# A pooling mixer's band products taken by source tile, its channel scale and shift applied behind them, its tables loaded one stage earlier, and router logits with the weights stationary

## The chip, the core and the metric

The kernel runs on one core of one Trainium2 chip. Its time is the device time of one execution in microseconds (us), as the median of several runs. TensorE is called PE in the profile's rows (PEld is its loading of stationary weights), VectorE is DVE, ScalarE is ACT, GpSimd is POOL and SyncE is SP; SPq, ACTq and POOLq are the instructions with which these engines issue transfers.

## What is computed

Two layers of a diffusion backbone work on 512 tokens of 1024 channels. Layer 0 is an attention and retention mixer, layer 1 a pooling mixer. Each mixer is followed by a mixture of 16 experts, of which every token takes two from one group. Everything is fp32. The parts that the change touches are these:

```python
def pool_mixer(h, pool_w, pool_scale):          # h = rms_norm(x, norm_mix_w) * (1 + scale) + shift
    cs = cumulative sum of h over the tokens
    for gi, w in enumerate((2, 4, 8, 16)):      # 256 channels each
        mean = (sl[:, hi] - sl[:, lo]) / (hi - lo)      # centred window of w tokens, cut at the ends
        groups.append(mean - h of these channels)
    mixed = jnp.einsum('btgc,gcd->btgd', pooled, pool_w).reshape(b, t, d)
    return mixed * pool_scale                   # x = x + g1 * mixed

def moe_route(flat, router_w, router_b):        # flat = modulate(rms_norm(x, norm_ffn_w), shift, scale)
    s = jax.nn.sigmoid((flat @ router_w).astype(jnp.float32))
    biased = s + router_b
    ...                                         # best group, its top two experts, their weights
```

## The kernel before

The program is a row of stages, and each ends with a barrier of all engines (`stage_over`). Inside a stage every engine works through its own list in the written order and waits for semaphores. The stages are: mixer of layer 0 with the routing front of its mixture (`front0`), mixture 0 (`moe(0)`), the pooling stage with `front1`, mixture 1 (`moe(1)`), and a last stage that adds the experts' results and applies the final norm.

In a mixture SP streams 48 matrices of expert weights in halves of 1 MB through a ring in SBUF (`put_half`), 414 GB/s while it runs. Its last half is issued long before the last expert is computed, and the experts' results go to a DRAM buffer (`y_scratch`) from ACT's queue.

The pooling stage does this. POOL issues eight indirect gathers (`Combine.fetch`, two per token tile of 128 rows, 512 KB each), and DVE adds each to the residual stream `x_res` (`Combine.add`, two operations per tile). ACT squares each tile and sums its squares, POOL makes the reciprocal root of it (`rstd_of`), and DVE applies it with the norm weight and the scale row and then adds the shift row (two operations per tile into `xhat`). The rows of scale, shift and norm weight are broadcast to all partitions. DVE then folds the gate row and `pool_scale` into the mixing weights `pool_w`. The pooling itself is a banded matrix of 512x512 per window, and PE multiplies with it: `xhat` is stationary, a 128x128 block of the band is moving. For each of 8 channel tiles k and each of 4 target tiles it takes the two or three source tiles that are near, 80 products in all, after a wait for all four tiles of `xhat`. Four PSUM banks are used in turn, and ACT copies each result to `pooledT`. The mixing products (`pool_w`, 32 of 256 columns) follow, DVE adds their results to `x_res`, and then `front1` runs.

A front (class `Front`) does for each tile: square on ACT, root on POOL, two operations of norm on DVE, 8 transposes on PE (`transposes`), one copy on ACT (`copy_T`, into `hT`), and 8 products with the router's weights (`logits`: 128 columns of `hT` are stationary and the 16 columns of `router_w` move). After the fourth tile ACT takes the sigmoid of a 128x64 block in PSUM (`scores`), which ends the stage. SP stores `xhat` to DRAM and loads the front's rows and tables and the first six halves of the next mixture's weights. The engine profile counts two records of PE for each fp32 product, and one for a transpose.

Two regions of SBUF have several uses: `shared` is one, and `arena` is what a stage takes beyond it.

## Time and profile before

| what | value |
|---|---|
| time, median of 3 runs | 1220.41 us (1220.31 to 1221.9) |
| the profiled execution: its time, and the span of its engines | 1222.1 us, 1220.2 us |
| share of the span in which engines are busy | PE 85%, PEld 66%, DVE 77%, ACT 50%, POOL 14% |
| mean granted clock of PE | 0.925 of full speed |
| mixture 0 begins, pooling stage begins | 458.69 us, 781.16 us |
| mixture 1 begins, last stage begins | 870.26 us, 1193.14 us |

The shares are means over stages of different kinds. In the two mixtures PE is busy nearly throughout. Between them lies a stretch of 89 us with a share of 2 to 3 tenths of PE in its first half. Times of single rows are counted from the span's start. The granted clock is 1.00 at 2.4 GHz and 0.50 at 1.2 GHz.

### The profile page before, as it was taken

How to read it: one execution, taken by the hardware profiler on the slowest of the kernel's cores; microseconds unless marked ns; L12 is line 12 of the kernel's file. 1: busy time of each engine (PE TensorE's matmuls, PEld its weight loads, DVE VectorE, ACT ScalarE, POOL GpSimd, SP SyncE). 2: the span in 40 equal slices, each digit the busy share in tenths (PEclk: the TensorE clock that was granted, in tenths of full speed). 3: DMA queues.
4: the chain of work that ended last, by engine and by line, in shares of the span. 5: the costliest groups of instructions: out<-in, count | busy, mean ns of one | idle time of the engine just before them, and what ended most of it. 6: DMA issues, size and time to landing. Idle time of an engine off the chain costs nothing. (4 is left out here: it accounts for less than half of the span.)

```text
span 1220.2 us, 13889 instructions
## 1 busy us (share of the span) xinstructions
PE 1039.8 (85%) x4830; PEld 802.0 (66%) x4830; DVE 935.0 (77%) x1042; ACT 605.2 (50%) x614; POOL 166.7 (14%) x172
## 2 busy tenths in 40 slices
PE   6789999997898983999999999239579999999970
PEld 1576767774565452788888888138558888888860
DVE  5578888964993337799999998273569999999955
ACT  1534222222663122777777776023347777777731
POOL 0100200000100004410000000221063211221005
PEclk9899999997999985999999999659579999999995
DMA  9625798555014024999999997494179999999936
GB/s 372 241 69 211 257 326 311 206 207 224 10 60 129 35 100 136 292 411 413 415 413 414 413 414 312 145 352 140 52 227 392 413 414 415 413 414 414 413 128 229
DMA packets 142861, 334.14 MB, mean 274 GB/s; under 512 B 10848, under 2 KB 12840, under 8 KB 142688
## 3 DMA queue, kind: packets, MB, share of 16 engines
q1 hardware_dynamic: 122936, 279.69, 60.5%
q10 hardware_dynamic: 12392, 28.68, 6.3%
q0 software_dynamic: 7488, 25.19, 5.4%
q8 instruction: 26, 0.43, 0.2%
q14 instruction: 19, 0.16, 0.0%
HBM read 310.42 MB, written 23.15 MB: 273 GB/s over the span
## 5 line engine op out<-in xcount | busy, mean ns | idle before, releaser
L1828 DVE TENSOR_TENSOR w_lo<-ring,w_hi 128x2048 fp32r<-128x2048 f32 x192 | 431.3, 2285 | 25.4 <-ACT w_hi L1674 22.1
L1674 ACT CAST w_hi<-ring 128x2048 fp32r<-128x2048 f32 x192 | 365.8, 1914 | 131.6 <-DMA ring<-in_moe_w_up 50.2
L1919 PE MATMUL bank<-w_hi,xT_hi 128*128 128x512 f32 x512 | 205.2, 401 | 8.1 <-DVE xT_lo L1835 8.1
L1919 PE MATMUL bank<-w_hi,xT_lo 128*128 128x512 f32 x512 | 201.5, 394 | 0.0
L1919 PE MATMUL bank<-w_lo,xT_hi 128*128 128x512 f32 x512 | 201.1, 393 | 0.0
L1368 PE MATMUL bank<-ring_last_parts,arena_parts 128*128 128x512 f32 (+1 forms) x320 | 117.7, 398 | 5.4 <-DVE ring_parts L988 2.7
L1919 PEld LDWEIGHTS bank<-w_hi,xT_hi 128*128 128x128 f32 x512 | 97.3, 190 | 29.4 <-DVE xT_lo L1835 9.8
L1919 PEld LDWEIGHTS bank<-w_hi,xT_lo 128*128 128x128 f32 x512 | 97.1, 190 | 21.2
L1919 PEld LDWEIGHTS bank<-w_lo,xT_hi 128*128 128x128 f32 x512 | 97.5, 190 | 19.4
L1046 DVE SCALAR_TENSOR_TENSOR gate_b<-ring,silu_c,gate_b 128x512 f32<-128x512 f32 x140 | 105.9, 756 | 4.5
L1934 PE MATMUL bank<-w_hi,hT_hi 128*128 128x512 f32 x256 | 101.2, 395 | 7.5 <-DVE w_lo L1828 7.5
L1934 PE MATMUL bank<-w_hi,hT_lo 128*128 128x512 f32 x256 | 100.8, 394 | 0.0
L1934 PE MATMUL bank<-w_lo,hT_hi 128*128 128x512 f32 x256 | 100.6, 393 | 0.0
L1368 PE MATMUL bank<-ring_parts,arena_parts 128*128 128x512 f32 (+1 forms) x256 | 100.6, 393 | 0.0
L1368 PEld LDWEIGHTS bank<-ring_last_parts,arena_parts 128*128 128x128 f32 x320 | 60.4, 192 | 31.6 <-issue 13.1
L1368 PE MATMUL bank<-ring_last_parts,x_parts 128*128 128x512 f32 x192 | 77.3, 403 | 0.0
L1631 POOL DMA_INDIRECT shared<-xh_scratch,shared x32 | 62.9, 1966 | 63.9 <-DVE shared L1819 55.8
L1934 PEld LDWEIGHTS bank<-w_hi,hT_hi 128*128 128x128 f32 x256 | 48.9, 191 | 18.1 <-issue 7.9
L741 ACT CAST ring_last_parts<-ring 128x1024 fp32r<-128x1024 f32 x24 | 25.2, 1050 | 68.7 <-PE bank L1368 63.1
L1661 POOL CAST shared<-shared 128x1 uint32<-128x1 int32 x26 | 11.2, 431 | 329.0 <-PE bank L1902 323.0
L1934 PEld LDWEIGHTS bank<-w_lo,hT_hi 128*128 128x128 f32 x256 | 48.9, 191 | 10.2
L1934 PEld LDWEIGHTS bank<-w_hi,hT_lo 128*128 128x128 f32 x256 | 48.6, 190 | 10.3
(246 smaller groups left out, 1425.5 us busy)
## 6 DMA issues: line engine op xcount, KB each, us to landing
ring<-in_moe_w_gate SPq DMA_DIRECT2D x64, 1024.0 KB, 11.5
ring<-in_moe_w_up SPq DMA_DIRECT2D x64, 1024.0 KB, 13.4
ring<-in_moe_w_down SPq DMA_DIRECT2D x64, 1024.0 KB, 11.1
ring<-in_ada_w SPq DMA_DIRECT2D x21, 2048.0 KB, 8.7
y_scratch<-shared ACTq DMA_DIRECT2D x32, 512.0 KB, 6.0
ring<-in_w_in ACTq DMA_DIRECT2D x21, 512.0 KB, 3.8
shared<-in_ada_w SPq DMA_DIRECT2D x2, 2048.0 KB, 16.0
x_res<-in_x SPq DMA_DIRECT2D x8, 512.0 KB, 12.4
```

The costliest lines, as they stand in the source:

```text
L741: nc.scalar.copy(w_high(n), w_raw(n)).then_inc(m_whi, 1)
L1046: ins = nc.vector.scalar_tensor_tensor(ada_acc[:, i % 2, :], w[:, k, :], silu_c[:, 0, k:k + 1], onto, ALU.mult, ALU.add)
L1368: last = pe.matmul(acc(u)[:, c0:c1], hs[h_], ws[w_], start=(kk == 0 and i == 0), stop=(kk == KD - 1 and i == 2))
L1631: pool.indirect_dma_start(out=xg[:, u, :], out_offset=None, in_=xh_dram, in_offset=bass.IndirectOffsetOnAxis(ap=idx[:, c:c + 1], axis=0)). ...
L1661: nc.gpsimd.tensor_copy(idx[:, u:u + 1], lists[:, m:m + 1]).then_inc(s_idx, 1)
L1674: nc.scalar.copy(w_hi[:, buf(u, p), :], half(raw(e, p))).then_inc(s_hi, 3 if isinstance(e, int) and (e, p) == (-1, 3) else 1)
L1828: V.tensor_tensor(w_lo[:, buf(u, p), :], half(raw(e, p)), w_hi[:, buf(u, p), :].bitcast(F32), ALU.subtract).then_inc(s_lo, 3 if isinstance ...
L1919: last = pe.matmul(bank[:, b, :], xs[:, kk, :], ws[:, k, :], start=(kk == 0 and i == 0), stop=(kk == KD - 1 and i == 2))
L1934: last = pe.matmul(bank[:, 6 + hf, :], xs[:, kk, :], ws[:, k, at], start=(kk == 0 and i == 0), stop=(kk == KE - 1 and i == 2))
```

## The change

The change has five parts.

1. The band products go by source tile. For each source tile t, as soon as its `xhat` is there, PE multiplies it, for each of the 8 channel tiles, with the 128 rows of the band that belong to it, 135 to 143 columns wide (`band_range`), and adds into eight PSUM banks. That makes 32 products.
2. The norm before them is one operation on ACT (`normed`, x times the reciprocal root). Scale, norm weight and shift act per channel, and channels are the partitions of the result, so they are applied where it is copied out of PSUM: four banks by ACT, four by DVE (`BY_ACT`, `BY_DVE`). The shift is multiplied with the mean column sum of the bands (`k_band_sum`).
3. Bands, raw `pool_w`, gate row and the three vectors in column form are loaded by SP at the end of mixture 0, into free parts of `shared` and `mod`. The column loads take elements of 4 bytes, 1024 of them in each of three. SP waits for all seven loads in that stage.
4. In the pooling stage DVE folds the gate before its adds, then does its eight adds in one run. SP loads the front's rows and tables before the six weight halves and not between them. PE puts the first transposes of the front ahead of the last mixing products, and runs logits(t) right behind transposes(t).
5. In both fronts the router's weights (16 columns) are stationary and 128 columns of `hT` move. The result lies by expert. ACT takes the sigmoid of 16x512, PE turns it back with four transposes (`scores_T`), and DVE copies 128x64 to `score` (`copy_scores`), which ends the stage.

```diff
+BAND_W = P + max(WINDOWS) - 1
+def band_range(t):
+    return max(t * P - (max(WINDOWS) // 2 - 1), 0), min((t + 1) * P + max(WINDOWS) // 2, SEQ)
...
             def scores(self, act):
                 act.wait_ge(self.lg, NT)
-                nc.scalar.activation(self.at.score..., bank[:, self.LOGITS, 0:NT * NE], ACT.Sigmoid).then_inc(self.done, 1)
+                nc.scalar.activation(self.by_expert, bank[0:NE, self.LOGITS, :], ACT.Sigmoid).then_inc(self.sg, 1)
+            def scores_T(self, pe):
+                pe.wait_ge(self.sg, 1)
+                for t in range(NT):
+                    last = pe.transpose(bank[:, self.SCORES, t * NE:(t + 1) * NE], self.by_expert[:, t * P:(t + 1) * P],
+                                        ident[0:NE, 0:NE])
+                last.then_inc(self.sgt, 1)
+            def copy_scores(self, dve):
+                dve.wait_ge(self.sgt, 1)
+                nc.vector.tensor_copy(self.at.score..., bank[:, self.SCORES, 0:NT * NE]).then_inc(self.done, 1)
...
                 for k in range(KD):
-                    last = pe.matmul(bank[:, self.LOGITS, t * NE:(t + 1) * NE], self.at.hT[:, k, t * P:(t + 1) * P],
-                                     self.at.router_w[:, k, :], start=(k == 0), stop=(k == KD - 1))
+                    last = pe.matmul(bank[0:NE, self.LOGITS, t * P:(t + 1) * P], self.at.router_w[:, k, :],
+                                     self.at.hT[:, k, t * P:(t + 1) * P], start=(k == 0), stop=(k == KD - 1))
...
# mixture 0, SP, behind the last halves of the expert weights
+                    if l == 0:
+                        sp.dma_start(bands..., a["k_bands"]).then_inc(s_pool, 16)
+                        sp.dma_start(pool_w_raw..., a["pool_w"][0]...).then_inc(s_pool, 16)
+                        sp.dma_start(gate1_b[:], mod_row(1, G1)).then_inc(s_pool, 16)
+                        for i, src in enumerate((mod_dram[1, SC1 * D:(SC1 + 1) * D], mod_dram[1, SH1 * D:(SH1 + 1) * D],
+                                                 a["norm_mix_w"][1])):
+                            sp.dma_start(pool_cols[:, i * KD:(i + 1) * KD], src.rearrange("(k p) -> p k", p=P)
+                                         ).then_inc(s_pool, 16)
+                        sp.dma_start(pool_cols[:, 3 * KD:3 * KD + 1], a["k_band_sum"]).then_inc(s_pool, 16)
+                        sp.wait_ge(s_pool, 16 * 7)
...
# pooling stage, SP
+                sp.dma_start(pool_scale, a["pool_scale"][0].partition_broadcast(P)).then_inc(p_ps, 16)
+                sp.wait_ge(p_wg, 1)
                 sp.wait_ge(combine.done, NT - 1)
...
                 front1.load_rows(sp)
                 front1.load_tables(sp)
+                sp.wait_ge(combine.done, NT)
+                for r in range(6):
                     put_half(sp, 1, 0, r)
...
# pooling stage, ACT: squares(0), squares(1), normed(0), squares(2), normed(1), squares(3), normed(2), normed(3), then
+                for k in BY_ACT:
+                    act.wait_ge(p_pl, K_ORDER.index(k) + 1)
+                    nc.scalar.activation(pooledT[:, k, :], bank[:, k, :], ACT.Identity, scale=scale_c[:, k:k + 1],
+                                         bias=shift_c[:, k:k + 1]).then_inc(p_ea, 1)
...
# pooling stage, DVE: the two column vectors, the gate, all adds, then
                 front1.scales(dve)
+                for k in BY_DVE:
+                    dve.wait_ge(p_pl, K_ORDER.index(k) + 1)
+                    nc.vector.tensor_scalar(pooledT[:, k, :], bank[:, k, :], scale_c[:, k:k + 1], shift_c[:, k:k + 1],
+                                            ALU.mult, ALU.add).then_inc(p_ed, 1)
...
# pooling stage, PE
-                pe.wait_ge(p_ld, 32)
-                pe.wait_ge(p_xh, NT)
-                for k in range(KD):
...
+                for t in range(NT):
+                    pe.wait_ge(p_xh, t + 1)
+                    lo, hi = band_range(t)
+                    for k in K_ORDER:
+                        last = pe.matmul(bank[:, k, lo:hi], xhat[:, t, k * P:(k + 1) * P], bands[:, k // 2, t, 0:hi - lo],
+                                         start=(t == 0), stop=(t == NT - 1), skip_group_check=True)
...
+                for t in range(3):
+                    mix(t)
+                front1.transposes(pe, 0)
+                mix(3)
+                front1.logits(pe, 0)
+                for t in range(1, NT):
                     front1.transposes(pe, t)
-                    if t >= 1:
-                        front1.logits(pe, t - 1)
-                front1.logits(pe, NT - 1)
+                    front1.logits(pe, t)
+                front1.scores_T(pe)
```

PE's list in the pooling stage, before; L2246 are band products, L2257 mixing products, L318 the transposes and L328 the logits of `front1`.

```order
L2246 MATMUL bank<-arena 128x128 x80
L2257 MATMUL bank<-arena 128x256 x32
L318 MATMUL bank<-ident,shared 128x128 x16
L328 MATMUL bank<-shared 128x16 x8
L318 MATMUL bank<-ident,shared 128x128 x8
L328 MATMUL bank<-shared 128x16 x8
L318 MATMUL bank<-ident,shared 128x128 x8
L328 MATMUL bank<-shared 128x16 x16
```

The same place in the changed program; L2284 are band products, L2300 mixing products, L343 transposes, L353 logits and L305 the transposes of the scores.

```order
L2284 MATMUL bank<-shared,arena 128x136 x8
L2284 MATMUL bank<-shared,arena 128x143 x16
L2284 MATMUL bank<-shared,arena 128x135 x8
L2300 MATMUL bank<-arena 128x256 x24
L343 MATMUL bank<-ident,shared 128x128 x8
L2300 MATMUL bank<-arena 128x256 x8
L353 MATMUL bank<-shared 16x128 x8
L343 MATMUL bank<-ident,shared 128x128 x8
L353 MATMUL bank<-shared 16x128 x8
```

The first transposes moved ahead of the last 8 mixing products, each tile's logits stand right behind its transposes, and 80 band products became 32.

DVE's list at the head of the pooling stage, before; L2119 are the adds, L2206 the scale row, L2212 and L2214 the norm, L2218 and L2221 the gate, L298 the front's scale row.

```order
L2119 SCALAR_TENSOR_TENSOR x_res<-shared,weight,x_res 128x1024 x4
L2206 SCALAR_TENSOR_TENSOR arena<-arena 128x1024
L2119 SCALAR_TENSOR_TENSOR x_res<-shared,weight,x_res 128x1024 x2
L2212 SCALAR_TENSOR_TENSOR arena<-x_res,rstd,arena 128x1024
L2214 TENSOR_TENSOR arena<-arena 128x1024
L2119 SCALAR_TENSOR_TENSOR x_res<-shared,weight,x_res 128x1024 x2
```

The same place in the changed program; L2252 and L2253 are the column vectors, L2255 and L2257 the gate, L2163 the adds, L323 the front's scale row and L2266 the copies out of PSUM.

```order
L2252 SCALAR_TENSOR_TENSOR mod<-mod 128x8
L2253 TENSOR_SCALAR mod<-mod 128x8
L2255 TENSOR_TENSOR gate_b<-gate_b,arena 128x1024
L2257 TENSOR_TENSOR arena<-shared,gate_b 128x4x256 x2
L2163 SCALAR_TENSOR_TENSOR x_res<-arena,weight,x_res 128x1024 x8
L323 SCALAR_TENSOR_TENSOR shared<-shared,arena 128x1024
L2266 TENSOR_SCALAR arena<-bank,mod 128x512 x4
```

The gate moved ahead of the adds, the four norms left DVE, and the front's scale row stands ahead of DVE's four copies.

## Rows read from the trace of the kernel before

**Rows 1.** Timeline, pooling stage: start, length, engine, line, operation, idle before.

```profile
781.16 0.34 SPq L2154 DMA_DIRECT2D arena<-mod_scratch  x1
791.24 1.28 DVE L2119 SCALAR_TENSOR_TENSOR x_res<-shared,weight,x_res 128x1024 f32<-128x1024 f32 x1 [15.61 <-DMA shared<-y_scratch,row_of]
801.19 1.06 ACT L2178 ACTIVATE arena<-x_res 128x1024 f32<-128x1024 f32 x1 [2.75 <-DVE x_res L2119]
802.70 1.44 POOL L212 TENSOR_TENSOR rstd<-rstd,minus_half 128x1 f32<-128x1 f32 x1
803.65 2.60 DVE L2119 SCALAR_TENSOR_TENSOR x_res<-shared,weight,x_res 128x1024 f32<-128x1024 f32 x2
812.51 1.23 DVE L2214 TENSOR_TENSOR arena<-arena 128x1024 f32<-128x1024 f32 x1
813.89 20.12 PE L2246 MATMUL bank<-arena 128*128 128x128 f32 x160 [39.51 <-DVE arena L2214]
834.05 0.59 ACT L2182 COPY arena<-bank 128x512 f32<-128x512 f32 x1 [1.65 <-PE bank L2246]
```

**Rows 2.** Timeline, mixing products and front, to mixture 1's first transfer.

```profile
834.68 14.08 PE L2257 MATMUL bank<-arena 128*128 128x256 f32 x64 [0.68 <-ACT arena L2182]
848.60 1.04 PE L318 MATMUL bank<-ident,shared 128*128 128x128 f32 x8
849.67 1.01 ACT L277 COPY shared<-bank 128x1024 f32<-128x1024 f32 x1 [5.37 <-PE bank L318]
861.73 6.85 PE L328 MATMUL bank<-shared 128*128 128x16 f32 x32
868.61 0.22 ACT L287 ACTIVATE shared<-bank 128x64 f32<-128x64 f32 x1 [4.11 <-PE bank L328]
870.26 0.32 SPq L1615 DMA_DIRECT2D gate_b<-mod_scratch  x1
```

**Rows 3.** Gathers of the pooling stage: issues first and last, time to landing.

```profile
L2104 POOL DMA_INDIRECT shared<-y_scratch,row_of x8: 933/938/940, 782.4 to 791.1; - x8
...
DMA to landing us min/median/max: 8.9/9.5/9.6
```

**Rows 4.** Gathers of the last stage, time to landing.

```profile
DMA to landing us min/median/max: 4.7/5.6/5.9
```

**Rows 5.** The last stage's only other load (512 KB, final norm weight), time to landing.

```profile
DMA to landing us min/median/max: 3.3/3.3/3.3
```

**Rows 6.** Windows: length, busy PE, PEld, DVE, ACT, POOL, clock, DMA share, GB/s.

```profile
444.50:447.20 2.70, 0.01 (x1) 0.00 (x0) 0.60 (x1) 2.05 (x3) 0.74 (x2) 1.00 0.00 0
447.20:449.20 2.00, 1.96 (x16) 1.86 (x16) 1.94 (x2) 0.00 (x0) 0.00 (x0) 1.00 0.00 0
813.80:818.00 4.20, 4.11 (x19) 4.14 (x20) 3.44 (x3) 0.00 (x0) 0.00 (x0) 0.50 1.05 405
848.70:855.30 6.60, 3.72 (x34) 3.41 (x32) 4.09 (x4) 4.12 (x6) 1.93 (x3) 1.00 0.19 79
855.30:858.00 2.70, 2.70 (x15) 2.70 (x16) 2.02 (x2) 1.01 (x1) 0.55 (x1) 0.57 0.47 194
```

**Rows 7.** Timeline, end of the first front: last logits and sigmoid.

```profile
452.89 3.59 PE L328 MATMUL bank<-shared 128*128 128x16 f32 x16 [1.10 <-ACT shared L277]
456.52 0.22 ACT L287 ACTIVATE shared<-bank 128x64 f32<-128x64 f32 x1 [2.17 <-PE bank L328]
```

**Rows 8.** Timeline, mixture 0: SP's last weight half, ACT's last store.

```profile
746.33 0.38 SPq L450 DMA_DIRECT2D ring<-in_moe_w_down  x1
...
775.67 0.34 ACTq L1694 DMA_DIRECT2D y_scratch<-shared  x1
```

**Rows 9.** Page, DMA issues: count, KB each, median us from issue to landing.

```profile
ring<-in_moe_w_down SPq DMA_DIRECT2D x64, 1024.0 KB, 11.1
```

**Rows 10.** DMA view, 825 to 827 us, tables of the front: packets by size.

```profile
DMA packets 1613, 0.44 MB, mean 222 GB/s; under 512 B 1411, under 2 KB 1542, under 8 KB 1613
```

**Rows 11.** Scatters of token numbers into the lists: 128 four-byte elements each.

```profile
DMA to landing us min/median/max: 2.6/8.9/12.5
```

More of the change, by code:

```diff
@@ L83, in constants @@
             full[t, t] -= 1.0
-        for b, (a, t) in enumerate([(0, 0), (1, 1), (NT - 1, NT - 1), (0, 1), (2, 1)]):
-            bands[:, g, b] = full[a * P:(a + 1) * P, t * P:(t + 1) * P]
+        band_sum += full.sum(0).mean()
+        for t in range(NT):
+            lo, hi = band_range(t)
+            bands[:, g, t, 0:hi - lo] = full[t * P:(t + 1) * P, lo:hi]
     rows = np.zeros((2, NE), np.float32)
@@ L94, in constants @@
         "k_ages": np.ascontiguousarray(ages.reshape(P, -1), np.float32),
-        "k_bands": bands.reshape(P, -1), "k_rows": rows, "k_token": np.ascontiguousarray(token),
+        "k_bands": bands.reshape(P, -1), "k_band_sum": np.full((P, 1), band_sum, np.float32), "k_rows": rows, "k_token": np.ascontiguousarray(token),
         "k_places": np.arange(P, dtype=np.float32)[None, :],
@@ L2123, in build_program @@
         moe(0)
-        stage_memory(14000 + 17000)
-        rows, at = carve(0, 2, NT, D)
-        combine = Combine("combine0", rows)
+        stage_memory(33500)
         normw_ffn, at = carve(14000, D)
@@ L2131, in build_program @@
         assert front1.at.end <= 14000
-        bands, at = carve(at, len(WINDOWS), 5, P)
+        rows, at = carve(at, 2, NT, D)
+        combine = Combine("combine0", rows)
         pool_w, at = carve(at, len(WINDOWS), 2, 2 * P)
@@ L2175, in _, with squares @@
             def _(act):
-                for t in range(NT):
+                def squares(t):
                     act.wait_ge(combine.done, t + 1)
@@ L2179, in _, with normed @@
                                          accum_out=stats[:, t:t + 1]).then_inc(p_sq, 1)
-                for k in range(KD):
-                    act.wait_ge(p_pl, k + 1)
-                    nc.scalar.copy(pooledT[:, k, :], bank[:, k % 4, :]).then_inc(p_plc, 1)
+                def normed(t):
+                    act.wait_ge(p_rs, t + 1)
+                    nc.scalar.activation(xhat[:, t, :], x[:, t, :], ACT.Identity, scale=rstd[:, t:t + 1]).then_inc(p_xh, 1)
+                squares(0)
+                squares(1)
+                normed(0)
+                squares(2)
+                normed(1)
+                squares(3)
+                normed(2)
+                normed(3)
+                act.wait_ge(p_cs, 1)
+                for k in BY_ACT:
+                    act.wait_ge(p_pl, K_ORDER.index(k) + 1)
+                    nc.scalar.activation(pooledT[:, k, :], bank[:, k, :], ACT.Identity, scale=scale_c[:, k:k + 1],
+                                         bias=shift_c[:, k:k + 1]).then_inc(p_ea, 1)
                 for t in range(NT):
@@ L2232, in _, with mix @@
                 front1.norm(dve, NT - 1)
+                front1.copy_scores(dve)
             @block.tensor
             def _(pe):
-                pe.wait_ge(p_ld, 32)
-                pe.wait_ge(p_xh, NT)
-                for k in range(KD):
-                    if k >= 4:
-                        pe.wait_ge(p_plc, k - 3)
-                    g = k // 2
-                    for t in range(NT):
-                        near = [(t2, b) for t2, b in ((t - 1, 3), (t, 0 if t == 0 else 2 if t == NT - 1 else 1), (t + 1, 4))
-                                if 0 <= t2 < NT]
-                        for n, (t2, b) in enumerate(near):
-                            last = pe.matmul(bank[:, k % 4, t * P:(t + 1) * P], xhat[:, t2, k * P:(k + 1) * P],
-                                             bands[:, g, b, :], start=(n == 0), stop=(n == len(near) - 1))
-                    last.then_inc(p_pl, 1)
-                pe.wait_ge(p_plc, KD)
-                pe.wait_ge(p_wg, 1)
-                for t in range(NT):
+                for t in range(NT):
+                    pe.wait_ge(p_xh, t + 1)
+                    lo, hi = band_range(t)
+                    for k in K_ORDER:
+                        last = pe.matmul(bank[:, k, lo:hi], xhat[:, t, k * P:(k + 1) * P], bands[:, k // 2, t, 0:hi - lo],
+                                         start=(t == 0), stop=(t == NT - 1), skip_group_check=True)
+                        if t == NT - 1:
+                            last.then_inc(p_pl, 1)
+                def mix(t):
+                    if t == 0:
+                        pe.wait_ge(p_wg, 1)
                     if t >= 2:
```

82 lines of the change are left out of this document (38 added, 44 removed).

## The prediction

> **What bounds the kernel now.** I read the page first: PE is busy in 85% of the span, and its slices dip twice, at the first front and in the stretch between the mixtures. Then I read the timeline of that stretch, since the change lies almost wholly in it. The pooling stage lasts from 781.16 to 870.26 [rows 1, 2], 89.1 us, and each step in it waits for the one before. The reader should follow it as a chain. The first gather's rows reach DVE at 791.24. DVE's adds are cut up by norms that wait for POOL, so that the last add ends at 803.65 + 2.60 = 806.25 and the last norm at 813.7. Only then does PE begin, after 39.51 us of idleness [rows 1]. The band products take 20.12 us, and the last copy out of PSUM starts when they end, at 834.05. The mixing products take 14.08 us, and from their end at 848.76 it is 20.1 us to the end of the sigmoid at 868.83 [rows 2]. Nothing in this stage covers anything else for long, so a shorter chain shortens the kernel. The weights of mixture 1 are no limit: they are loaded in the same stage, and mixture 1 starts only at the barrier.
>
> The windows show PE's clock [rows 6]. It is granted at 0.50 while the band products begin, for 4.1 us, and the products behind them take half as long each. It is full until 855.3 and falls in the front's tail, before 858. In the first front PE did nothing from 444.5 to 447.2 and still had the full clock, and again in the next window with its 16-column products; the last products there, 16 records in 3.59 us, ran slow (224 ns each against 123) [rows 6, 7].
>
> **The change part by part**, as times on the old time axis.
>
> *Adds.* The load of `pool_scale` lands 3.3 us after its issue if it is like the last stage's lone load [rows 5]: 784.5. Three gate operations of 1.23 us (the 128x1024 operation of DVE in rows 1) end at 788.2. The old stage loads three rows beside its gathers, the new one loads one, as the last stage does; there the gathers land after 4.7 to 5.9 us instead of 8.9 to 9.6 [rows 3, 4]. So the first is there at 787.1 to 788.3, and the last, issued at 791.1, at 797.0. Eight adds of 1.30 us [rows 1] run from 788.3 to 798.7, and the gate is hidden in the wait for the gathers. If the gathers landed as late as before, the last add would end at 791.1 + 9.6 + 1.3 = 802.0. I take the first, since the traffic is that of the last stage.
>
> *Norm.* Per tile ACT squares (1.06 us and 0.19 to read the sum) and applies the root (no row has this operation; the square has its shape and one input, so 1.06; the copy of 1.01 [rows 2] is the lower end). POOL's root takes 0.19 + 1.44 us [rows 1]. ACT interleaves them, and with POOL busy issuing until 792 to 794.5 the four tiles are ready at about 797.4, 799.6, 801.8 and 803.7, the last one 10 us sooner than before.
>
> *Band products.* 160 records were made for 80 products. In the slow window 19 take 4.11 us, 216 ns each; the other 141 take 16.0 us, 113 ns each [rows 1, 6]. A product of 139 columns in the mean instead of 128 costs two records times 1.09: 0.47 us slow, 0.25 fast, so 8 of them 3.8 or 2.0. Tile 0 runs slow from 797.4 to 801.2. If the clock rises 4.1 us after the start, as it did, tile 1 ends at 803.4, tile 2 at 805.4 and tile 3 at 807.4. A rise one tile later costs 1.7. Copies go on ACT and DVE side by side: 0.59 for a bank on ACT [rows 1], half of 1.23 on DVE. Two of them fit beside two products, so the mixing products start at about 807.4, where they started at 834.68: 27.3 us gained. DVE's copies stand behind the front's scale row, which waits for three loads issued at about 796.5. At 3.3 us they cost nothing, at the 9.6 of a crowded queue 807 + 1.3 = 808.3 is the first copy's start, 2.5 us late. I take 0.
>
> *Mixing products.* 14.1 us as before, but the first transposes now stand ahead of the last eight. They wait for add 1 (1.2) and norm 0 (two operations, 2.5) behind the second tile's products, which end at 814.6: ready at 818.6, where PE has been free since 818.0. With 1.04 for themselves they add 1.7. The mixing ends at 823.2, 25.6 us sooner than before.
>
> *Tail.* Logits now move 128 columns, 8 products of 2 x 113 ns, 1.8 us; the old ones took 1.96 for 16 records and were set by loading 128 columns of weights (PEld 1.86 of 2.00) [rows 6]. So at full clock the swap itself is worth almost nothing. A round is transposes 1.04 with 0.25 until ACT sees them, copy 1.01, hand-over 0.1, logits 1.8: 4.2 us. Logits 0 and three rounds end at 823.2 + 1.8 + 12.6 = 837.6. Then come the new steps: a sigmoid of 512 columns for 64 (at most the bank copy's 0.59), four transposes (half of 1.04), a copy of 128x64 (0.22 as on ACT, at least nothing), and three hand-overs of 0.1: 1.6 us. The barrier took 870.26 - 868.83 = 1.4. The stage ends at 840.6, a gain of 29.7.
>
> *The clock in the tail.* This sum has PE at full clock to the end. What stood before both falls in the old trace were products of 16 moving columns; both are gone. A pause alone did not lower it from 444.5 to 447.2. The Trainium skill, "TensorE: Matmul & The Clock Gate", Part 1, has the clock fall after an idle window. By that rule too it would stay up here, since no pause of PE in a round is longer than 1.4 us; but the old tail fell without long idleness, so the rule alone is not enough.
>
> *First front.* Old: the last logits began at 452.89 after a pause of 1.10, so the transposes ended at 451.8 and, slow, took about twice 1.04 from 449.7; slow logits 3.59, sigmoid until 456.74 [rows 7]. New at full clock: transposes to 450.8 (the norm before them ends when it did), copy to 451.9, logits 1.8 and hand-over to 454.0, new steps 1.6: 455.6. That gains 1.1. At the slow clock nothing is saved and the new steps cost 1.5.
>
> *Tables in mixture 0.* SP's last weight half is issued at 746.33 [rows 8] and lands after 11.1 us [rows 9]: 757.4. Behind it come 2.74 MB, 6.8 us at 405 GB/s [rows 6]: 764.2. The column loads are 3,200 packets of 4 bytes, 200 for each of 16 DMA engines. In two microseconds of the front's tables 1,411 small packets went through [rows 10], 22.7 ns per packet and engine: 4.5 us, so 768.7. ACT issues its last store at 775.67 [rows 8], and the barrier comes later still. The loads are hidden behind the last expert with 7 us to spare, up to 57 ns per packet. The other end is the scatter of four-byte elements: 8 packets per engine in 8.9 us [rows 11], 1.1 us each, 222 us in all. That is a software queue's whole latency and not a packet's cost, and I stay with the tables. The Trainium skill, "DMA: Bandwidth & Descriptors", Specifications, says that below 512 B a write becomes read-modify-write and misses line rate. It gives no price that I use; the rule speaks for a packet dearer than mine, and its effect is the late-tables rival.
>
> *Mixture 1.* Its six halves are issued after the last add, behind 1.8 MB of rows and tables, from about 803. 8 MB at 405 GB/s is 20 us: 823, and the barrier is at 840. Its inside does not change.
>
> **Sum.** 29.7 + 1.1 = 30.8, less 0.5 for a clock that may rise late: 30.3. The profiled execution took 1222.1 with a span of 1220.2; the median of the runs, 1220.41, is 1.7 below it, and the gain is taken from the median: 1190.
>
> **Rivals.**
> - Clock falls in the tail. Each of three rounds then costs 2.0 for 1.04 and 3.5 for 1.8, 2.6 more, with the last transposes 8.2 in all, and the first front loses 1.5 instead of gaining 1.1. Time 1200.5, or 1194 and up if it falls late. For it: PE still pauses 1.4 us in each round. Against it: fuller products. Chance 0.15.
> - DVE or loads late (gathers as slow as before, or the scale row's loads at 9.6 us): 2.5 to 3.5 more, 1193 to 1194. Chance 0.11.
> - Tables late but bearable: 60 to 200 ns per packet hold the barrier of mixture 0 for 1 to 28 us, 1191 to 1218. Chance 0.03.
> - No gain: the weights of mixture 1 would have to land as late as 870. Nothing in the rows says so. Chance 0.005.
> - Slower than before: four-byte packets above 57 + 30,300/200 = 209 ns. At the scatter's 1.1 us the tables would end at 986 and the time be near 1400. Chance 0.005.
> - The forecast, 1186 to 1193, has the rest, 0.70.
>
> **How the numbers follow.** About 0.2% (2.4 us) is what a measurement here can tell from no change. All likely cases are beyond it: faster 0.985, same 0.005, slower 0.01. The range takes in the forecast, late loads and most of the clock case: 1185.5 to 1198. It leaves out the deepest slow tail and late tables.
>
> **What the new trace would show.** Right: DVE's adds in one run ending near 799; PE's first band product near 797; mixing from 807 to 823; logits records of about 113 ns to the end with clock 1.00; stage end near 840; mixture 0's end unmoved at 781. Wrong if PE sits before the mixing for DVE's scale row, if the last logits take 3.5 us per tile, or if SP holds the barrier of mixture 0.

## The result: 29.6 us faster, as forecast

| kernel | median us (lowest to highest, runs) | ratio to before, 95% interval |
|---|---|---|
| before | 1221.16 (1220.31 to 1222.41, 4) | |
| changed | 1191.53 (1190.79 to 1191.72, 4) | 0.976 [0.9746, 0.9774] |

The forecast was 1190.0 and its range 1185.5 to 1198. The profiled execution has a span of 1189.6 us, where before had 1220.2, and a mean granted clock of 0.939. PE's line on the page:

```profile
PE 1025.7 (86%) x4742; PEld 781.1 (66%) x4742; DVE 929.3 (78%) x1041; ACT 607.9 (51%) x614; POOL 137.7 (12%) x172
```

The stages, each counted from its first transfer to that of the next, show where the time came from:

| stage | before, us | changed, us | gain |
|---|---|---|---|
| up to mixture 0 | 458.69 | 456.68 | 2.0 |
| mixture 0 | 322.47 | 323.51 | -1.0 |
| pooling stage with the front | 89.10 | 58.94 | 30.2 |
| mixture 1 | 322.88 | 323.78 | -0.9 |
| last stage | 27.06 | 26.69 | 0.4 |

The first row and the two mixtures differ between profiles of kernels that are the same there: mixture 0 began between 456.68 and 459.80 us in the eleven profiles with the new logits and took 322.34 to 323.55 us. So only the third row is clear of that scatter. It divides into three parts:

| pooling stage | before, us | changed, us | gain |
|---|---|---|---|
| stage begins to first band product | 32.73 | 15.48 | 17.25 |
| first band product to first mixing product | 20.79 | 11.17 | 9.6 |
| first mixing product to the stage's end | 35.58 | 32.29 | 3.3 |

The timeline of the changed pooling stage, first half, answers to [rows 1]. Columns are start, length, engine, line, operation and the idle time before it.

```profile
784.58 1.23 DVE L2255 TENSOR_TENSOR gate_b<-gate_b,arena 128x1024 f32<-128x1024 f32 x1 [4.04 <-DMA arena<-in_pool_scale]
...
788.12 10.66 DVE L2163 SCALAR_TENSOR_TENSOR x_res<-arena,weight,x_res 128x1024 f32<-128x1024 f32 x8
...
790.67 0.94 POOL L2148 DMA_INDIRECT arena<-y_scratch,row_of  x1 [0.30 <-issue]
790.79 1.06 ACT L2211 ACTIVATE arena<-x_res 128x1024 f32<-128x1024 f32 x1 [26.50 <-DVE x_res L2163]
...
792.31 1.52 POOL L222 TENSOR_TENSOR rstd<-rstd,minus_half 128x1 f32<-128x1 f32 x1
...
794.49 1.13 ACT L2216 ACTIVATE arena<-x_res,rstd 128x1024 f32<-128x1024 f32 x1
...
795.67 10.73 PE L2284 MATMUL bank<-shared,arena 128*128 128x136 f32 x64 [22.29 <-ACT arena L2216]
...
801.59 1.22 DVE L323 SCALAR_TENSOR_TENSOR shared<-shared,arena 128x1024 f32<-128x1024 f32 x1 [2.81 <-DMA arena<-in_norm_ffn_w]
...
804.90 2.79 ACT L2229 ACTIVATE arena<-bank,mod 128x512 f32<-128x512 f32 x4 [2.84 <-PE bank L2284]
805.16 2.97 DVE L2266 TENSOR_SCALAR arena<-bank,mod 128x512 f32<-128x512 f32 x4 [2.35 <-PE bank L2284]
...
806.84 10.60 PE L2300 MATMUL bank<-arena 128*128 128x256 f32 x48 [0.43 <-DVE arena L2266]
```

The eight adds are one row without a gap, so no gather made DVE wait. PE starts 15.5 us after the stage begins, where before it took 32.7. While PE works through the band products, ACT's norms of the later tiles go on beside it. DVE's idle time of 2.81 us ahead of L323 looks like a late load, but it costs nothing: DVE would otherwise have waited for PE's banks, which it does right behind, for 2.35 us.

The second half answers to [rows 2]; L353 are the logits, L305 turns the scores back.

```profile
817.75 1.09 PE L343 MATMUL bank<-ident,shared 128*128 128x128 f32 x8 [0.32 <-DVE shared L334]
...
818.68 3.62 PE L2300 MATMUL bank<-arena 128*128 128x256 f32 x16
818.88 1.01 ACT L289 COPY shared<-bank 128x1024 f32<-128x1024 f32 x1 [2.46 <-PE bank L343]
...
822.23 1.92 PE L353 MATMUL bank<-shared 128*16 128x128 f32 x16
...
826.28 1.92 PE L353 MATMUL bank<-shared 128*16 128x128 f32 x16 [1.10 <-ACT shared L289]
...
834.37 1.92 PE L353 MATMUL bank<-shared 128*16 128x128 f32 x16 [1.10 <-ACT shared L289]
...
836.33 0.59 ACT L299 ACTIVATE shared<-bank 16x512 f32<-16x512 f32 x1 [0.49 <-PE bank L353]
...
836.97 0.41 PE L305 MATMUL bank<-ident,shared 16*128 16x16 f32 x4 [0.68 <-ACT shared L299]
837.42 0.22 DVE L312 COPY shared<-bank 128x64 f32<-128x64 f32 x1 [6.66 <-PE bank L305]
...
839.13 0.32 SPq L1648 DMA_DIRECT2D gate_b<-mod_scratch  x1
```

Each round of the tail repeats after 4.05 us: transposes, a wait of 1.10 for ACT's copy, logits. The logits keep 1.92 us to the last, where the old tail ended with 32 records in 6.85 us [rows 2]. The windows of the changed kernel give the clock (columns as in [rows 6]):

```profile
796.00:801.00 5.00, 5.00 (x23) 5.00 (x23) 2.61 (x3) 4.38 (x7) 2.98 (x5) 0.50 0.79 255
801.00:802.00 1.00, 1.00 (x8) 1.00 (x7) 0.41 (x1) 1.00 (x1) 0.00 (x0) 0.71 1.01 341
...
822.30:836.30 14.00, 10.69 (x89) 8.38 (x88) 6.15 (x5) 5.57 (x7) 0.74 (x2) 1.00 0.27 109
```

It is half for the first 5.9 us of band products (0.71 in the second window puts the rise at 801.6) and full through the whole tail.

### The profile page after: what moved, and what is told of

Read it like the earlier page. It is cut to its first block and busy times, and to the rows that moved or that the text cites. A ratio compares the mean times of both kernels' runs of the same rounds, so it can differ in the third digit from the quotient of the medians.

```text
span 1189.6 us, 13716 instructions
## 1 busy us (share of the span) xinstructions
PE 1025.7 (86%) x4742; PEld 781.1 (66%) x4742; DVE 929.3 (78%) x1041; ACT 607.9 (51%) x614; POOL 137.7 (12%) x172
## 5 line engine op out<-in xcount | busy, mean ns | idle before, releaser
L1896 DVE TENSOR_TENSOR shared<-bank,gate_b 128x1024 f32<-128x1024 f32 x32 | 39.0, 1219 | 21.1 <-PE bank L1978 21.1
L1394 PEld LDWEIGHTS bank<-ring_parts,arena_parts 128*128 128x128 f32 x256 | 48.5, 189 | 8.6
```

Source lines behind the costliest of these rows:

```text
L1394: last = pe.matmul(acc(u)[:, c0:c1], hs[h_], ws[w_], start=(kk == 0 and i == 0), stop=(kk == KD - 1 and i == 2))
L1896: V.tensor_tensor(y_sb[:, u, :], bank[:, 6:8, :].rearrange("p b c -> p (b c)"), gate2_b[:], ALU.mult).then_inc(s_y, 1)
```

## The experiments

Ratios are to the kernel before, which ran on the same chip beside them: 1221.42 us for the one with the gate behind the adds, the last version and the repeat, 1220.39 for the other four of the first five, 1220.24 for the rest. "Stage" is the pooling stage, 89.10 us before and 58.94 changed. Differences of a few us are read from it, since the rest of the program varies by one to three microseconds from one profile to the next. The stage has a scatter of its own: the clock rose 3.3 to 5.9 us after the first band product, 5.9 in the changed kernel's profile and 4.4 in its repeat, whose stage is 58.07 us. From the first mixing product to the stage's end both take 32.29 us. Where an edit lies in that part, this shorter count is given too, as the length from the mixing on.

### The logits form in the kernel before

```diff
 # kernel before, Front.logits
-    last = pe.matmul(bank[:, self.LOGITS, t * NE:(t + 1) * NE], self.at.hT[:, k, t * P:(t + 1) * P],
-                     self.at.router_w[:, k, :], start=(k == 0), stop=(k == KD - 1))
+    last = pe.matmul(bank[0:NE, self.LOGITS, t * P:(t + 1) * P], self.at.router_w[:, k, :],
+                     self.at.hT[:, k, t * P:(t + 1) * P], start=(k == 0), stop=(k == KD - 1))
 # and scores, scores_T, copy_scores as in part 5
```

> The kernel before with part 5 alone: router weights stationary in both fronts, sigmoid by expert, four transposes and a copy behind it; the rest is as before. Theory A (the old 16-column products are what let PE's clock fall and kept it low until the end; the new ones do not): in front 1 the last 32 records of logits take 3.6 us instead of 6.85, the stage ends 3 to 4 us sooner although the new steps cost 1.6, and with the first front the kernel gains 4 to 5 us, near 1216. Theory B (the clock follows PE's pauses whatever the products): it falls at the same place but climbs back sooner, gain 1 to 3 us. Theory C (the form of the products does nothing to the clock): two fronts pay 1.2 to 1.6 us each for the new steps, 2.5 to 3 us slower than before.

Measured: 1216.53 us, ratio 0.9968 [0.9957, 0.9979]; stage 84.82, 4.3 us shorter. Its tail and a window over it:

```profile
858.20 3.67 PE L343 MATMUL bank<-shared 128*16 128x128 f32 x32
```

```profile
848.00:862.00 14.00, 10.83 (x91) 8.56 (x89) 5.95 (x5) 7.73 (x11) 2.48 (x4) 1.00 0.27 112
```

The last 32 records take 3.67 us for 6.85, at a clock that stays at 1.00 in this tail. Here L343 is the line of the logits. The order of PE's list is that of before and it waits for the same engines, so in this tail the form of the logits keeps the clock. The length from the mixing on is 31.40 us for 35.58. One profile could owe this to chance, but the mean granted clock of all ten executions is 0.932 to 0.936, where the thirteen of the kernel before beside them have 0.922 to 0.929.

### The changed kernel with the old logits

```diff
-    last = pe.matmul(bank[0:NE, self.LOGITS, t * P:(t + 1) * P], self.at.router_w[:, k, :],
-                     self.at.hT[:, k, t * P:(t + 1) * P], start=(k == 0), stop=(k == KD - 1))
+    last = pe.matmul(bank[:, self.LOGITS, t * NE:(t + 1) * NE], self.at.hT[:, k, t * P:(t + 1) * P],
+                     self.at.router_w[:, k, :], start=(k == 0), stop=(k == KD - 1))
 # scores as before; scores_T and copy_scores gone
```

> The changed kernel without part 5: 128 columns of hT stationary again, sigmoid straight to the scores. Theory A: the clock falls in the tail of the pooling stage once the 16-column products begin, the last rounds run at 0.50, and the kernel is 4 to 7 us slower than the changed one (1196 to 1198). Theory C: it saves the new steps in both fronts and is 2 to 3 us faster than the changed one (about 1189).

Measured: 1193.46 us, ratio 0.9783 [0.9764, 0.9802]; stage 61.61, 2.7 us longer than the changed kernel's. The last logits and the windows over the tail:

```profile
836.30 3.60 PE L340 MATMUL bank<-shared 128*128 128x16 f32 x16 [1.10 <-ACT shared L289]
```

```profile
822.00:826.00 4.00, 2.90 (x26) 2.66 (x26) 3.07 (x3) 1.96 (x3) 0.00 (x0) 1.00 0.28 113
826.00:829.00 3.00, 2.71 (x18) 2.31 (x17) 1.92 (x2) 0.35 (x3) 0.74 (x2) 0.68 0.40 165
829.00:840.00 11.00, 8.98 (x40) 8.47 (x40) 0.59 (x1) 3.32 (x5) 0.00 (x0) 0.50 0.12 49
```

With 16 moving columns the clock falls and does not come back, though the pauses are the same 1.10 us. The length from the mixing on is 35.65 us, 3.4 longer. The two experiments confirm each other: in all eleven profiles with the new logits the last logits of this tail ran at full clock, and in both with the old ones at half. The mean granted clock of the four executions here is 0.929 to 0.930, of the changed kernel's four 0.937 to 0.939. The price is smaller than the 4 to 7 us that I expected. The clock fell only between 826 and 829, with part of the tail done, and the old form needs no steps that turn the scores back.

### The tables loaded in the pooling stage

```diff
 # mixture 0, SP: the seven loads and their wait are gone
 # pooling stage, SP, behind pool_scale
+    sp.dma_start(gate1_b[:], mod_row(1, G1)).then_inc(p_gt, 16)
+    sp.dma_start(pool_w_raw..., a["pool_w"][0]...).then_inc(p_gt, 16)
+    sp.dma_start(bands..., a["k_bands"]).then_inc(p_bd, 16)
+    # the three column loads and k_band_sum: p_col
 # DVE
     dve.wait_ge(p_ps, 16)
+    dve.wait_ge(p_gt, 32)           # gate and pool_w, ahead of the adds
+    # behind the adds: dve.wait_ge(p_col, 16 * 4), then the two column vectors
 # PE, ahead of the band products
+    pe.wait_ge(p_bd, 16)
```

> The changed kernel with the seven table loads issued at the start of the pooling stage, behind pool_scale, instead of at the end of mixture 0. Theory 1 (the early load is worth its place): 2.2 MB of gate, weights and bands share the queues with the gathers, the gate is folded and the adds start 3 us later, the band products wait for bands; 3 to 6 us slower than the changed kernel, 1195 to 1197. Theory 2 (the loads were hidden anyway, as DVE has 8 us of idleness there): within 1 us. If the extra 1.0 us of mixture 0 comes from the table loads, mixture 0 is back at 322.5 us here; if it comes from the clock's phase it need not be.

Measured: 1206.81 us, ratio 0.9885 [0.9863, 0.9908]; stage 75.61, so 16.7 us longer where I expected 3 to 6. This was a miss of mine:

```profile
801.99 1.23 DVE L2252 TENSOR_TENSOR gate_b<-gate_b,arena 128x1024 f32<-128x1024 f32 x1 [26.89 <-DMA shared<-in_pool_w]
```

The gate stands ahead of DVE's adds, and it waits for `pool_w` until 801.99. Everything behind it is late by that much. Mixture 0 without the loads is no shorter (323.55 us).

### Those tables, with the gate behind the adds

The miss left open whether the place of the gate costs the 16.7 us or the transfers themselves.

```diff
 # previous kernel, DVE
+    for t in range(NT):
+        combine.add(dve, t)
     dve.wait_ge(p_ps, 16)
     dve.wait_ge(p_gt, 32)
     ...                              # gate, pool_w
-    for t in range(NT):
-        combine.add(dve, t)
```

> The kernel of run e3 (all tables loaded in the pooling stage) with DVE folding the gate behind its eight adds instead of ahead of them, since in e3 the adds waited 27 us for the weights. If e3's 16.7 us were mostly the gate standing in front of the adds, the adds now end near 803 when the shared queues are empty, the mixing starts near 810, and the kernel comes out near 1195 to 1198. If it was the transfers themselves, it stays above 1203.

Measured: 1202.47 us, ratio 0.9845 [0.9829, 0.9861]; stage 70.79.

```profile
790.10 1.28 DVE L2152 SCALAR_TENSOR_TENSOR x_res<-arena,weight,x_res 128x1024 f32<-128x1024 f32 x1 [14.64 <-DMA arena<-y_scratch,row_of]
...
804.75 9.46 PE L2285 MATMUL bank<-shared,arena 128*128 128x136 f32 x64 [30.55 <-DMA shared<-k_bands]
...
814.77 1.22 DVE L323 SCALAR_TENSOR_TENSOR shared<-shared,arena 128x1024 f32<-128x1024 f32 x1 [5.23 <-DMA arena<-in_norm_ffn_w]
...
817.79 4.51 PE L2301 MATMUL bank<-arena 128*128 128x256 f32 x12 [3.58 <-DVE arena L2266]
```

Three waits for transfers take the place of one: the adds come singly, each behind its gather; PE waits for the bands until 804.75; and DVE's scale row, ahead of its copies, comes late, so that the mixing waits until 817.79. Behind that pause of 3.58 us the clock fell, to 0.50 from 819 to 821, and the 48 records of mixing took 12.29 us for 10.60. The time lies between my two forecasts, 1195 to 1198 and above 1203, so neither was right. Of the 16.7 us, 4.8 are the gate's place and 11.9 the transfers, 1.7 of these by the clock; each is sure to about a microsecond, the scatter of the clock's rise. That is what the loads in mixture 0 are worth with this order of work.

### Twelve more column loads in mixture 0

```diff
+    for i in range(12):
+        spare, _ = carve(9968 + i * KD, KD)
+        sp.dma_start(spare, mod_dram[1, SC1 * D:(SC1 + 1) * D].rearrange("(k p) -> p k", p=P)).then_inc(s_pool, 16)
-    sp.wait_ge(s_pool, 16 * 7)
+    sp.wait_ge(s_pool, 16 * 19)
```

> The changed kernel with 12 more column loads of 1024 elements of 4 bytes each behind the three, into words that nobody reads. It prices a four-byte packet. At 22.7 ns per packet and DMA engine (the prediction's price) they add 17 us of transfers, which end near 780, some 2 to 4 us behind the barrier's old place: 1193 to 1196. At 53 ns (3.4 us per load, the time SP spent on issuing one) they add 41 us, the barrier of mixture 0 moves by 25 us: about 1216.

Measured: 1191.82 us, ratio 0.9772 [0.9752, 0.9793]; stage 58.98, mixture 0 323.44 us. First the changed kernel, issues of SP and ACT at the end of mixture 0, then the windows of the experiment:

```profile
744.27 0.38 SPq L475 DMA_DIRECT2D ring<-in_moe_w_down  x1
...
745.68 9.33 SPq L1664 DMA_DIRECT2D gate_b<-mod_scratch  x1
...
755.06 3.49 SPq L1667 DMA_DIRECT2D mod<-mod_scratch  x2
758.59 3.36 SPq L1667 DMA_DIRECT2D mod<-in_norm_mix_w  x1
...
774.68 0.34 ACTq L1738 DMA_DIRECT2D y_scratch<-shared  x1
```

```profile
767.00:769.00 2.00, 2.00 (x6) 1.61 (x5) 0.15 (x1) 0.00 (x0) 0.00 (x0) 0.50 0.83 6
769.00:771.00 2.00, 2.00 (x6) 1.55 (x5) 0.00 (x0) 0.00 (x0) 0.00 (x0) 0.51 0.70 5
771.00:773.00 2.00, 2.00 (x10) 1.60 (x10) 0.00 (x0) 0.00 (x0) 0.00 (x0) 1.00 0.23 2
```

The DMA engines are busy for 0.7 to 0.8 of the time while 5 or 6 GB/s move: these are the packets of 4 bytes. 12,288 of them, 768 for each engine, run between 761 and 772 us. That is at most some 14 ns each, where I had reckoned 22.7; SP issued the twelve loads in 9.31 us, so its issue may be the limit. Both my prices, and with them both forecasts, were too high. Even five times the column loads end ahead of the barrier, and the kernel's time does not change.

### Band products after all four norms

```diff
+    pe.wait_ge(p_xh, NT)
     for t in range(NT):
-        pe.wait_ge(p_xh, t + 1)
         lo, hi = band_range(t)
```

> The changed kernel, but PE waits for all four tiles of xhat before its first band product; nothing else is changed. If what part 1 gives is the overlap of products with norms, PE starts at about 802.2 instead of 795.7, pays its 4 us at the low clock after that, and the mixing starts 5 to 6 us later: 1196 to 1198. If the gain is only in the number of products (32 for 80) and the start does not matter, since another wait ends last before the mixing, it stays within 1 us of the changed kernel.

Measured: 1197.45 us, ratio 0.9814 [0.9792, 0.9837]; stage 65.13, 6.2 us longer. PE's first band product comes 22.1 us into the stage instead of 15.5:

```profile
803.16 5.19 PE L2284 MATMUL bank<-shared,arena 128*128 128x136 f32 x21 [28.89 <-ACT arena L2216]
```

The mixing begins 32.8 us into the stage for 26.7 in the changed kernel and 25.8 in its repeat. So the overlap of norms and band products is worth 6 to 7 of the 30 us. Here nothing overlaps, and from the first band product to the first mixing product it is still 10.75 us for the 20.79 of before. So some 10 us come from the smaller number of products and the copies on two engines. No run takes these two apart or alone; the figure is read from the rows.

### The norm on DVE

```diff
 # DVE, in place of ACT's normed(t): after add(t + 2)
+    dve.wait_ge(p_rs, t + 1)
+    nc.vector.tensor_scalar(xhat[:, t, :], x[:, t, :], rstd[:, t:t + 1], None, ALU.mult).then_inc(p_xh, 1)
```

> The changed kernel with the one-operation norm on DVE, between its adds as before, and ACT only squaring. If moving the norm to ACT is a part of the gain, DVE again waits for POOL's root between adds, the last tile of xhat is 2 to 4 us late and the time is 1193 to 1195. If ACT was the bound there (2.2 us per tile against DVE's 2.6 for two adds), it is within 1 us.

Measured: 1191.8 us, ratio 0.977 [0.9747, 0.9793]; stage 58.97, the same. On DVE the operation takes 0.76 us, on ACT 1.13. PE began 1.2 us later than in the changed kernel (16.7 us into the stage), but the clock rose 3.5 us after that and not 5.9, and the mixing began at the same 26.7. Against the repeat, which began it at 25.8, it is 0.9 late. So moving the norm to ACT gained less than a microsecond, if anything. That it became one operation probably gained more, since two of 1.28 and 1.22 us stood in its place; no run shows that alone.

### PE's old order in the tail

```diff
-    for t in range(3):
-        mix(t)
-    front1.transposes(pe, 0)
-    mix(3)
-    front1.logits(pe, 0)
-    for t in range(1, NT):
+    for t in range(NT):
+        mix(t)
+    for t in range(NT):
         front1.transposes(pe, t)
-        front1.logits(pe, t)
+        if t >= 1:
+            front1.logits(pe, t - 1)
+    front1.logits(pe, NT - 1)
```

> The changed kernel with PE's old order in the mixing and front: all four mixing tiles, then transposes(t) and logits(t-1) in turn. Theory 1 (the new order of part 4 buys 2 us or more by letting ACT's copy and the squares go sooner): 1193.5 or more. Theory 2 (what it gives by the early copy it loses again, since transposes in the mixing cost 1.1 to 1.7 us and PE pauses 1.1 us per round for ACT's copy, where the old order has the logits of the tile before): within 1 us of the changed kernel, 1190.5 to 1192.5.

Measured: 1189.64 us, ratio 0.9751 [0.9728, 0.9773]; stage 57.64, 1.3 us shorter than the changed kernel's.

```profile
806.72 14.05 PE L2300 MATMUL bank<-arena 128*128 128x256 f32 x64 [0.43 <-DVE arena L2266]
...
831.56 3.67 PE L353 MATMUL bank<-shared 128*16 128x128 f32 x32
```

Mixing runs unbroken, and the logits of one tile lie in the wait for the copy of the next. The order that came with part 4 costs 0.9 us: the length from the mixing on is 31.35 here and 32.29 in both profiles of the changed kernel. The rest of the 1.3 us by the stages is the clock's earlier rise in the band products. The medians agree in sign (1.9 us, below both my ranges), but they come from two chips, and the intervals of the ratios overlap. The first experiment, with the same order and the same logits, has nearly the same length (31.40).

### Two pairs of banks for the transposes

```diff
 # Front: odd tiles of front1 transpose into banks 4 and 5
+    def t_bank(self, t):
+        return 4 if self.l and t % 2 else 0
 # transposes
-    if t >= 1:
-        pe.wait_ge(self.hta, t)
+    if t >= (2 if self.l else 1):
+        pe.wait_ge(self.hta, t - 1 if self.l else t)
 # ACT: the square of tile 3 ahead of the copy of tile 1
 # PE: mix 0 to 2, transposes 0, mix 3, logits 0, transposes 1, then transposes(t), logits(t - 1), and logits 3
```

> The changed kernel with the rounds of front 1 taken apart: odd tiles are transposed into the mixing's banks 4 and 5, so that transposes no longer wait for ACT's copy; PE does logits(t-1) behind transposes(t); ACT squares tile 3 ahead of its copy of tile 1. If the tail is a round trip PE to ACT to PE of 4.05 us per tile, the last logits end 2 to 3 us sooner: 1188.5 to 1189.5. If DVE's norms (2.5 us per tile and an add) bound it, less than 1 us.

Measured: 1188.59 us, ratio 0.9745 [0.9722, 0.9768]; stage 56.64, 2.3 us shorter, and the length from the mixing on is 30.03 for 32.29. The ratios alone do not tell it from the changed kernel.

```profile
826.73 1.09 PE L349 MATMUL bank<-ident,shared 128*128 128x128 f32 x8 [0.90 <-DVE shared L339]
...
829.99 1.09 PE L349 MATMUL bank<-ident,shared 128*128 128x128 f32 x8 [0.32 <-DVE shared L339]
```

The wait for the copy is gone. The transposes of the last two tiles now wait for DVE's norm.

### The same, with all mixing products first

```diff
-    for t in range(3):
+    for t in range(NT):
         mix(t)
     front1.transposes(pe, 0)
-    mix(3)
-    front1.logits(pe, 0)
     front1.transposes(pe, 1)
+    front1.logits(pe, 0)
 # ACT: squares 0, 1, 2 ahead of the first copy
```

> Run e7 with all four mixing tiles ahead of the first transposes (what e6 showed to be the better order) and the square of tile 2 ahead of the copy of tile 0: mixing ends near 821, tile 3's norm 2.5 us later than tile 2's, last logits near 832.5 instead of 834.6. Expected 1186 to 1187.5; if DVE's chain of add and norm per tile still sets the end as in e7, no better than e7 (1188.6).

Measured: 1187.73 us (1184.33 to 1190.78, 5 runs), ratio 0.9718 [0.9704, 0.9733]; stage 55.64, length from the mixing on 28.88. The median is just above my range. The changed kernel was run once more beside it:

> The changed kernel itself once more, on the same chip as the two above, to compare them without the scatter between chips: ratio 0.976 to the kernel before, as in the first measurement; its first front and the last expert of mixture 0 may show the low clock at other places, which moves the time by 1 us.

Measured: 1190.3 us (1190.12 to 1193.19, 5 runs), ratio 0.9757 [0.9743, 0.977]; stage 58.07. The intervals do not touch. This version is 0.4% faster than the changed kernel, 2.6 us by the medians, 2.4 by the stages and 3.4 by the length from the mixing on (its clock rose late in the band products, after 5.7 us), and its median is the lowest of the study.

## Why the prediction was right, point by point

Times here are from the start of the pooling stage, which was 781.16 on the axis of the prediction and 780.19 in the changed trace.

| step | predicted | measured |
|---|---|---|
| gate begins | 3.3 | 4.4 |
| last add ends | 17.5 | 18.6 |
| first band product | 16.2 | 15.5 |
| mixing begins | 26.2 | 26.7 |
| mixing ends | 42.0 | 42.1 |
| one round of the tail | 4.2 | 4.05 |
| from the last logits to the barrier's end | 3.0 | 2.8 |
| stage | 59.4 | 58.9 |

- **Adds.** `pool_scale` took 1.1 us longer to land than the last stage's lone load [rows 5], and the whole run moved by that. The step that mattered, gathers as early as in the last stage [rows 4], held: they landed after 6.0 us (median of eight), and the adds ran without a gap.
- **Norm.** The square and the norm of the first tile were done sooner than I reckoned, since POOL had issued its last gather at 791.61 and began the root at once, where I had it busy until 792 to 794.5. ACT's norm took 1.13 us for the estimated 1.06. PE began 0.7 us sooner and then stood at the low clock for 5.9 us where I had 4.1, so nothing was left of it. This is the late rise for which the sum had 0.5 us. In the repeat it came after 4.4 us, and the mixing began at 25.8.
- **Mixing.** The first transposes ahead of the last eight products were ready at 817.75; PE had closed its 24 products (48 records) at 817.44. A record of the mixing products takes 0.22 us as before. The interruption cost 1.4 us (15.46 for 14.05), where I had 1.7.
- **Tail.** Three rounds at 4.05 instead of 4.2 give the half microsecond by which the stage is shorter than predicted. The new steps behind the logits are as estimated: 0.59, 0.41 and 0.22 us of work and the hand-overs. That the clock stays up was the step with the most doubt, with a chance of 0.15 against it. The first two experiments show that in this tail the form of the logits decides it, in this order of PE's list and in the old one.
- **First front.** The term that was mis-sized. Transposes of the third tile to the barrier took 15.21 us before and 14.70 in the changed kernel, a gain of 0.5 and not 1.1. After a pause of 2.72 us the clock did fall here, and it came back behind the new logits:

```profile
445.74 2.81 PE L353 MATMUL bank<-shared 128*16 128x128 f32 x16 [2.72 <-ACT shared L289]
448.48 1.81 PE L343 MATMUL bank<-ident,shared 128*128 128x128 f32 x8
...
451.40 1.92 PE L353 MATMUL bank<-shared 128*16 128x128 f32 x16 [1.10 <-ACT shared L289]
...
453.36 0.59 ACT L299 ACTIVATE shared<-bank 16x512 f32<-16x512 f32 x1 [0.49 <-PE bank L353]
```

  Logits of 2.81 and transposes of 1.81 us are slow ones, the last 1.92 is at full clock, where the last of before took 3.59 [rows 7]. In the kernel with PE's old order, whose first front is the same, the pause was 2.72 us too and the clock did not fall, and the stretch took 13.81. In the one with two bank pairs it took 15.42. So this gain lies between -0.2 and 1.4 us. Of the eleven profiles with the new logits four kept the clock in this front (13.81 or 13.82 us), and in seven it fell, in four behind the pause of 2.72 us and in three behind the one of 1.10 (14.40 to 15.42 us). In both with the old logits it fell. So the new form, which kept the clock in every tail, does not keep it here. The other 1.5 us of the 2.0 up to mixture 0 lie ahead of the changed code. The same pause of 2.72 us thus let the clock fall in some profiles and not in others. The Trainium skill, "TensorE: Matmul & The Clock Gate", Part 1, says that the gate's phase is not tied to the kernel, so that the same program meets it at different places from run to run; these profiles agree with that. The same part ties the fall to idleness. That rule alone, as the prediction said, is not enough: in the second experiment it fell with pauses of 1.10 us, and the tail of the first experiment has longer ones (up to 1.53) and full clock. In the old tail it fell in the transposes behind a pause of 1.69 us, which took 1.64 us for 1.06 (kernel before):

```profile
855.28 1.64 PE L318 MATMUL bank<-ident,shared 128*128 128x128 f32 x8 [1.69 <-DVE shared L309]
```

- **Tables.** Mixture 0 hides them with more room than I gave: the last column load has landed at 763.9 and the last small table at 765.3, not 768.7, and both table rivals are excluded up to five times the column loads. SP's issue of the gate row took 9.33 us (L1664 above), presumably because the transfers ahead of it filled the queue. It costs nothing, since SP has nothing else to do.
- **Mixtures.** I had their inside unchanged, but each was a microsecond longer in the changed trace. The windows over mixture 0 and over its last expert, of the changed kernel and then of its repeat:

```profile
456.68:780.19 323.51, 291.83 (x1354) 242.30 (x1354) 283.64 (x244) 213.66 (x145) 37.67 (x39) 0.94 0.92 354
763.00:771.00 8.00, 6.15 (x15) 4.87 (x16) 3.90 (x2) 1.29 (x1) 0.00 (x0) 0.57 0.21 66
```

```profile
457.55:779.89 322.34, 290.65 (x1354) 241.52 (x1354) 283.58 (x244) 215.53 (x145) 59.62 (x39) 0.95 0.93 355
763.00:771.00 8.00, 4.97 (x16) 4.05 (x17) 5.08 (x4) 1.90 (x1) 0.00 (x0) 0.79 0.23 66
```

  The same program needs 323.51 or 322.34 us. PE's busy time differs by 1.18 us in the whole mixture and by as much in these 8 us of the last expert, where the clock is at 0.57 or at 0.79: it comes back sooner or later behind a pause. The kernel without the loads in mixture 0 had 323.55, so they are not the cause. Why the clock takes the one or the other course stays open, and so does the 0.9 us of mixture 1, which takes 322.75 to 323.50 us in the twelve other profiles (323.29 in the repeat). None of it is shown to belong to the change's work.
- **Median.** Taking the gain from the median of the runs was fair: by spans it is 30.6, by medians 29.6. That the total came so near is in part luck: 1.5 us gained ahead of the changed code and 1.9 lost in the mixtures, none of them in my sum, nearly cancel, and so do PE's early start and the late clock.

The rivals: loads late, tables late and no gain did not come. The clock rival is real as a mechanism: the old logits bring it on in the changed order too (second experiment), and the new ones did in none of eleven profiles of this tail.

## What to carry to other kernels

In a stage that is one chain, add up the chain and not the engines' work: here PE's start moved by 17 us and the stage shrank by 30. The experiments put 6 to 7 us to working tile by tile and 12 to 17 to having the tables there beforehand, each taken out alone, so these are not terms of one sum. When an operation is put early in an engine's list, ask what it waits for: the gate ahead of the adds is free with its tables loaded and costs 5 us without. Then look once more at the order of the new tail, since here the old one was better by about a microsecond, and a second pair of banks with it by 2.4 to 3.4. And compare small changes from a point behind the clock's rise, since that rise alone moved the mixing's start by 0.8 us between two profiles of one kernel.

## What the runs showed of the hardware

- In the tail of the pooling stage the granted clock of a pausing PE went with the form of the products between the pauses. With 128 moving columns and 16 stationary ones it stayed at 1.00 over 14 us with 10.69 us busy, with 128 stationary and 16 moving it fell to 0.50 and stayed there for 11 us with 8.98 us busy. In the first front the same new form kept the clock in four profiles of eleven.
- The clock rose 3.3 to 5.9 us after the first band product (thirteen profiles with 32 or 80 products; 4.4 and 5.9 in two profiles of one kernel).
- Loads in elements of 4 bytes cost at most some 14 ns per packet on each DMA engine, and SP about 0.8 us for a load of 1,024 of them (twelve in 9.31 us), up to 3.4 us behind the large tables.
- Six further transfers beside eight gathers (gate row, `pool_w`, bands, three column loads; a seventh was issued behind them) stretched the gathers' adds from one run of 10.66 us to 15.56 us (790.10 to 805.66).
